# The sums of a modulation, once by VectorE over rows, once by TensorE over tiles

## The chip, the cores and the metric

One of the eight cores of a Trainium2 chip runs one launch of a layer of a streaming encoder, in fp32. The metric is the device time in microseconds (us) of a launch. The median of three runs of the kernel before is 1193.38 us.

## The reference

The layer has a token mixer (a convolution beside a gated recurrence) and a feed-forward part. Each is led by a normalisation whose shift and scale depend on a condition vector `c`. S = D = 1024, so that x has 8 x 8 tiles of 128 x 128.

```python
cond = jax.nn.silu(c)
mod = cond @ w_ada[l] + b_ada[l]          # 1024 -> 6 x 1024
sh1, sc1, gt1, sh2, sc2, gt2 = jnp.split(mod, 6)
h = rms_norm(x, g_pre_mix[l]) * (1.0 + sc1) + sh1
zin = h @ w_in[l]                         # 1024 x 1024 by 1024 x 3072
...
x = x + gt1 * rms_norm(mix, g_post_mix[l])
h2 = rms_norm(x, g_pre_ffn[l]) * (1.0 + sc2) + sh2
x = x + gt2 * rms_norm((silu(gate) * up) @ w_ffn_out[l], g_post_ffn[l])
```

The change is about `sh1` and `sc1`, 2 x 1024 sums of 1024 products each, for which 8 MB of `w_ada` are read.

## The kernel before

The program is written engine by engine, in one block; the order on every engine is that of its code, and semaphores are counted up between the engines. Every projection is made of three fp32r matmuls in place of one: weights and activations are split into a high and a low half (`w_hi`, `w_lo`, `ha_hi`, `ha_lo`, and `hb_` for the second half of the channels), and hi x hi, lo x hi and hi x lo are summed.

**The prologue** (until about 72 us) normalises x, transposes it, applies scale and shift, splits the result and makes the first two chunks of the input projection at the same time. It goes by sixteen groups: a group is a tile kt of 128 channels and a half of the tokens, in the order of `GROUPS` (line 71). For each of them

- TensorE transposes four tiles of x (`turn_x`, line 1443),
- ScalarE applies scale and shift out of PSUM into one of two buffers (line 663, the tile shows as `ggb`) and copies the high half (line 667),
- VectorE takes the low half (`low_half`, line 963), and
- TensorE makes six matmuls of 512 columns with it (`project_group`, line 1458).

TensorE's order is written out at the end of the tensor block: the transposes run three groups ahead of the projections.

**Scale and shift** come in four blocks of 256 channels. SyncE loads a block in four pieces of 512 KB (`load_block`, line 427) into a ring of three, so that the fourth block waits until the first is used. VectorE holds row p of channel group j on partition p: `sum_rows` multiplies the 512 values of a row j (256 shifts, 256 scales) by `cond[:, j]` and adds them up over j (lines 937 and 940), in two sums that line 945 adds (`acc_ready`). Then only the sum over the 128 partitions is left: `mod_sums(kt)` does it on TensorE with two matmuls against a column of ones (line 1430), for shift and scale of tile kt, and VectorE adds the bias and makes `gs` and `mod` from it (`scale_shift`, lines 952 and 954). VectorE's order is written out by hand, the pieces of `sum_rows` between the low halves.

**Others that look at these sums**: SyncE (the fourth block), and GpSimd, whose third split of weights (`split_at(2)`, lines 510 and 512) waits for the last block's sum. SyncE's later weight loads wait for the splits (line 396). GpSimd and SyncE then wait for the sixteenth group.

**Behind the prologue** TensorE makes the other chunks of the input projection (line 1495), with the heads' small matmuls and transposes between them, then the output projection and the feed-forward part (lines 1603 and 1680). The other four parts of the modulation are made there, on ScalarE and GpSimd, and summed over partitions by `column_sums` (line 1407); the change does not touch them.

Of the kernel before, what the change touches and what calls it, by code (L numbers as in the profile page):

```python
# [17 lines left out]
F32 = mybir.dt.float32  # L18
# [3 lines left out]
ALU = mybir.AluOpType  # L22
# [4 lines left out]
P = 128  # L27
D = 1024
S = 1024
KT = D // P  # L30
TT = S // P
# [38 lines left out]
ADA_RING = 3  # L70
# [69 lines left out]
def build(nc, t_in, out):  # L140
# [9 lines left out]
    with ctx:  # L150
        def sem(name):
            return ctx.enter_context(nc.semaphore(name))

        def group(specs):

            made = []
            with ExitStack() as place:
                for name, shape, dt in specs:
                    made.append(place.enter_context(nc.sbuf_tensor(name, shape, dt)))
            return made  # L160

        def keep(name, shape, dt=F32):
# [4 lines left out]
        ones = keep("ones", [P, P])  # L167
# [6 lines left out]
        cond = keep("cond", [P, KT])  # L174
# [20 lines left out]

        x0, ada0, acc0 = group([("x0", [P, TT, D], F32), ("ada0", [P, ADA_RING, KT, 2, 2 * P], F32),
                                      ("acc0", [P, 2, 2, 4 * P], F32)])
        qk, f, tt, vt, v, pmat, kdt, state, on, ot, y4, og, ada, acc, sg, u = group([
# [17 lines left out]
        def bank(i):  # L216
            return pair[i // 2][:, (i % 2) * HALF:(i % 2 + 1) * HALF]
# [12 lines left out]
        ada0_loaded = [sem(f"ada0_loaded{i}") for i in range(KT)]  # L230
        acc_ready = sem("acc_ready")
        full0_ready = sem("full0_ready")
# [157 lines left out]
        def _(sp):  # L390
# [31 lines left out]
            def load_block(b):  # L422
                if b >= ADA_RING:
                    sp.wait_ge(acc_ready, b - ADA_RING + 1)
                for q in range(4):
                    rows, s_ = slice(q // 2 * 4, q // 2 * 4 + 4), q % 2
                    sp.dma_start(ada0[:, b % ADA_RING, rows, s_, :], columns[:, rows, s_, b * 2 * P:(b + 1) * 2 * P]
                                 ).then_inc(ada0_loaded[2 * b + q // 2], 16)
# [54 lines left out]
        def _(pool):  # L483
# [51 lines left out]
            for g in range(2):  # L535
                split_at(g)
            pool.wait_ge(acc_ready, KT // 2)
            split_at(2)
# [355 lines left out]
        def _(dve):  # L894
# [33 lines left out]

            def sum_rows(b, rows):

                for j in rows:
                    src = ada0[:, b % ADA_RING, j, :, :].rearrange("p s n -> p (s n)")
                    dst = acc0[:, b % 2, j % 2, :]
                    if j % 4 == 0:
                        dve.wait_ge(ada0_loaded[2 * b + j // 4], 32)
                    if j < 2:
                        i_ = dve.tensor_scalar(dst, src, cond[:, j:j + 1], None, ALU.mult)
                    else:
                        me.wait(behind=1)
                        i_ = dve.scalar_tensor_tensor(out=dst, in0=src, scalar=cond[:, j:j + 1], in1=dst,  # L940
                                                      op0=ALU.mult, op1=ALU.add)
                    me.done(i_)
                if rows[-1] == KT - 1:
                    me.wait()
                    dve.tensor_tensor(acc0[:, b % 2, 0, :], acc0[:, b % 2, 0, :], acc0[:, b % 2, 1, :], ALU.add
                                      ).then_inc(acc_ready, 1)

            def scale_shift(kt):
# [22 lines left out]
            dve.wait_ge(cond_ready, 1)  # L971
            sum_rows(0, range(KT))
            for i in range(4):
# [5 lines left out]
            for i in range(5, TT):  # L979
                normalise_x(i)  # L980
            low_half(0)
            low_half(1)
            sum_rows(1, range(2))
            low_half(2)
            sum_rows(1, range(2, 4))
            low_half(3)
            sum_rows(1, range(4, KT))
            sum_rows(2, range(2))
            scale_shift(2)
            scale_shift(3)  # L990
            sum_rows(2, range(2, 4))
            low_half(4)
            sum_rows(2, range(4, 6))
            low_half(5)
            sum_rows(2, range(6, KT))
            low_half(6)
            scale_shift(4)
            low_half(7)
            sum_rows(3, range(3))
            scale_shift(5)  # L1000
            low_half(8)
            sum_rows(3, range(3, 6))
            low_half(9)
            sum_rows(3, range(6, KT))
            low_half(10)
            scale_shift(6)
            low_half(11)
            scale_shift(7)
            for g in range(12, 16):
# [385 lines left out]
        def _(pe):  # L1395
# [27 lines left out]
            def mod_sums(kt):  # L1423

                pe.wait_ge(acc_ready, kt // 2 + 1)
                if kt >= 2:
                    pe.wait_ge(full0_ready, 2 * kt - 3)
                for s_ in range(2):
                    first = s_ * 2 * P + kt % 2 * P
                    i_ = pe.matmul(bank(4 + 2 * (kt % 2))[:, s_:s_ + 1], acc0[:, kt // 2 % 2, 0, first:first + P],  # L1430
                                   ones[:, 0:1], start=True, stop=True)
                i_.then_inc(mod0_summed, 1)
# [352 lines left out]
```

## Time and profile before

| | |
|---|---|
| median of three runs | 1193.38 us (1192.98 to 1196.18) |
| profiled execution | 1198.91 us, span 1197.2 us |
| TensorE busy (matmuls) | 1149.7 us, 96% of the span |
| TensorE busy (weight loads) | 958.4 us, 80% |
| VectorE busy | 740.3 us, 62% |
| ScalarE, GpSimd busy | 306.0 us, 662.0 us |
| matmul records | 5528 |

The profiled execution has a time of its own, 1.7 us more than its span. TensorE counts as busy while a matmul runs, and matmuls overlap, so its busy share says little of its speed; the granted clock of a stretch (1.00 is 2.4 GHz, 0.50 is 1.2 GHz) stands beside it. A wait is put down to the instruction that ended it. The names in the profile are those of the tiles without their numbers: `ada` is `ada0`, `acc` is `acc0`, `pair` is PSUM.

### The profile page before, as it was taken

How to read it: one execution, taken by the hardware profiler on the slowest of the kernel's cores; microseconds unless marked ns; L12 is line 12 of the kernel's file. 1: busy time of each engine (PE TensorE's matmuls, PEld its weight loads, DVE VectorE, ACT ScalarE, POOL GpSimd, SP SyncE). 2: the span in 40 equal slices, each digit the busy share in tenths (PEclk: the TensorE clock that was granted, in tenths of full speed). 3: DMA queues.
4: the chain of work that ended last, by engine and by line, in shares of the span. 5: the costliest groups of instructions: out<-in, count | busy, mean ns of one | idle time of the engine just before them, and what ended most of it. 6: DMA issues, size and time to landing. Idle time of an engine off the chain costs nothing.

```text
span 1197.2 us, 13774 instructions
## 1 busy us (share of the span) xinstructions
PE 1149.7 (96%) x5528; PEld 958.4 (80%) x5528; DVE 740.3 (62%) x892; ACT 306.0 (26%) x459; POOL 662.0 (55%) x388
## 2 busy tenths in 40 slices
PE   2799999999999999999999999999999999999996
PEld 2678888888887888877888888888888888888875
DVE  6765988979988655658644444444444444444447
ACT  5355244272341624341110101010101010101014
POOL 4036433342433460324486868686868686868655
PEclk9999999999999999999999999999999999999988
DMA  9534323232310153211112121212120212121234
GB/s 331 165 123 141 97 87 93 81 102 71 104 37 24 49 206 110 88 36 53 36 34 72 34 73 35 71 35 72 34 72 27 79 35 72 35 71 35 71 116 184
DMA packets 94097, 98.52 MB, mean 82 GB/s; under 512 B 2925, under 2 KB 80978, under 8 KB 94034
## 3 DMA queue, kind: packets, MB, share of 16 engines
q1 hardware_dynamic: 92576, 93.33, 24.7%
q10 hardware_dynamic: 1458, 4.31, 0.9%
q8 instruction: 44, 0.72, 0.3%
q14 instruction: 19, 0.16, 0.0%
HBM read 89.25 MB, written 8.39 MB: 82 GB/s over the span
## 4 chain that ended last, share of the span: by engine, by line
PE 91%; DVE 5%; ACT 1%; SPq 1%; issue 1%; DMA 1%; ACTq 0%; DVEq 0%
PE pair L1680 30%; PE pair L1603 27%; PE pair L1495 22%; PE pair L1531 3%; PE pair L1458 1%; PE pair L1660 1%; DVE yt L1306 1%; DVE acc L940 1%; DMA x<-in_x 1%; SPq L396 1%; PE pair L1545 1%; PE pair L1526 1%; PE pair L1419 1%; PE pair L1407 1%; DVE yt L1310 1%
## 5 line engine op out<-in xcount | busy, mean ns | idle before, releaser
L1062 DVE SCALAR_TENSOR_TENSOR pair<-u,conv_w_col,pair 128x512 f32<-128x512 f32 x240 | 162.4, 747 | 1.2
L1360 DVE TENSOR_TENSOR yt<-yt,pair 128x1024 f32<-128x1024 f32 x80 | 97.6, 1220 | 101.8 <-PE pair L1603 101.2
L596 POOL TENSOR_TENSOR w_lo<-raw,w_hi 128x1024 fp32r<-128x1024 f32 x66 | 146.6, 2221 | 5.3
L594 POOL CAST w_hi<-raw 128x1024 fp32r<-128x1024 f32 x66 | 69.1, 1046 | 123.3 <-PE pair L1603 52.5
L517 POOL TENSOR_TENSOR w_lo<-raw,w_hi 128x1024 fp32r<-128x1024 f32 x21 | 52.4, 2496 | 106.3 <-ACT w_hi L681 106.3
L1603 PE MATMUL pair<-w_hi,u_hi 128*128 128x512 f32 x352 | 109.1, 391 | 0.0
L1603 PE MATMUL pair<-w_lo,u_hi 128*128 128x512 f32 x352 | 108.8, 390 | 0.0
L1603 PE MATMUL pair<-w_hi,u_lo 128*128 128x512 f32 x352 | 108.7, 390 | 0.0
L596 POOL TENSOR_TENSOR w_lo<-sraw,w_hi 128x1024 fp32r<-128x1024 f32 x38 | 104.2, 2742 | 3.0
L594 POOL CAST w_hi<-sraw 128x1024 fp32r<-128x1024 f32 x38 | 39.4, 1038 | 117.8 <-PE pair L1603 116.1
L528 POOL TENSOR_TENSOR acc<-acc,ada 128x1024 f32<-128x1024 f32 x28 | 67.3, 2403 | 52.4 <-ACT ada L725 51.1
L866 ACT ACTIVATE u_hi<-ufull 128x1024 fp32r<-128x1024 f32 x22 | 23.3, 1061 | 270.9 <-PE pair L1603 228.9
L1680 PE MATMUL pair<-t_hi,w_hi 128*128 128x512 f32 x228 | 88.7, 389 | 0.0
L1680 PE MATMUL pair<-t_lo,w_hi 128*128 128x512 f32 x228 | 88.7, 389 | 0.0
L1680 PE MATMUL pair<-t_hi,w_lo 128*128 128x512 f32 x228 | 88.7, 389 | 0.0
L1603 PEld LDWEIGHTS pair<-w_hi,u_hi 128*128 128x128 f32 x352 | 66.3, 189 | 14.0 <-DVE yt L1358 0.4
L1603 PEld LDWEIGHTS pair<-w_lo,u_hi 128*128 128x128 f32 x352 | 66.4, 188 | 13.9
L1603 PEld LDWEIGHTS pair<-w_hi,u_lo 128*128 128x128 f32 x352 | 66.3, 188 | 13.9
L1495 PE MATMUL pair<-ha_hi,w_hi 128*128 128x512 f32 x208 | 69.0, 413 | 4.2 <-ACT gate L842 2.3
L1495 PE MATMUL pair<-hb_hi,w_hi 128*128 128x512 f32 x208 | 68.1, 408 | 0.0
L1495 PE MATMUL pair<-ha_lo,w_hi 128*128 128x512 f32 x208 | 65.2, 395 | 0.0
L1495 PE MATMUL pair<-ha_hi,w_lo 128*128 128x512 f32 x208 | 65.0, 394 | 0.0
(255 smaller groups left out, 2591.1 us busy)
## 6 DMA issues: line engine op xcount, KB each, us to landing
ada<-in_w_ada SPq DMA_DIRECT2D x48, 512.0 KB, 4.0
raw<-in_w_ffn_in SPq DMA_DIRECT2D x44, 512.0 KB, 3.9
raw<-in_w_in SPq DMA_DIRECT2D x24, 512.0 KB, 3.9
raw<-in_w_ffn_out SPq DMA_DIRECT2D x22, 512.0 KB, 3.4
x<-in_x SPq DMA_DIRECT2D x8, 512.0 KB, 8.4
raw<-in_w_out SPq DMA_DIRECT2D x8, 512.0 KB, 3.4
x<-in_x SPq DMA_DIRECT2D x4, 1024.0 KB, 8.3
out<-x ACTq DMA_DIRECT2D x8, 512.0 KB, 2.6
```

Of the source, the lines that this page charges most:

```text
L396: sp.dma_start(raw[:, g % RAW, :] if src.shape[1] != KT else raw[:, g % RAW, :].rearrange("p (kt c) -> p kt c", kt=KT), src).then_inc(raw_ ...
L517: pool.tensor_tensor(w_lo[:, g % WS, :], raw[:, g % RAW, :], w_hi[:, g % WS, :], ALU.subtract).then_inc(w_split, 1)
L528: pool.tensor_tensor(acc[:, :], acc[:, :], ada[:, n % 2, :], ALU.add).then_inc(ada_added, 1)
L594: me.done(pool.tensor_copy(w_hi[:, g % WS, cols], src[:, cols]))
L596: pool.tensor_tensor(w_lo[:, g % WS, cols], src[:, cols], w_hi[:, g % WS, cols], ALU.subtract).then_inc(w_split, 1)
L866: act.activation(u_hi[:, e % 2, :], ufull[:, :], ACT.Copy).then_inc(uhi_ready, 1)
L1062: i_ = dve.scalar_tensor_tensor(out=dst, in0=src, scalar=w, in1=dst, op0=ALU.mult, op1=ALU.add)
L1360: dve.tensor_tensor(yt[:, i, :], yt[:, i, :], pair[2 + i % 2][:, :], ALU.add).then_inc(y_added, 1)
L1495: i_ = pe.matmul(dst[:, cols], w, x[:, cols], start=first and s_ == 0, stop=last and s_ == 2)
L1531: i_ = pe.matmul(dst[0:rows, i * 64:(i + 1) * 64], qk[:, 1, i * P:i * P + rows], right(qk[:, 0, cols(i)], 1 << half), start=True, stop=True)
L1603: i_ = pe.matmul(dst[:, cols], x, w[:, cols], start=first and s_ == 0, stop=last and s_ == 2)
L1680: i_ = pe.matmul(dst, a, x[:, n, :], start=n == 0 and s_ == 0, stop=n == 3 and s_ == 2)
```

## The change

`sum_rows` goes, and with it the tile `acc0` and the semaphore `acc_ready`. `mod_sums(kt)` now reads the loaded block itself: for the shift and for the scale of tile kt it adds up eight matmuls in PSUM, one for each j, with the 128 x 128 tile of `ada0` as weights and the column `cond[:, j]` moving. It waits for the block's loads in place of `acc_ready`. The fourth load and GpSimd's third split wait for `mod0_summed`, that is for TensorE. The two other steps of VectorE keep their order.

```diff
             def load_block(b):
                 if b >= ADA_RING:
-                    sp.wait_ge(acc_ready, b - ADA_RING + 1)
+                    sp.wait_ge(mod0_summed, 2 * (b - ADA_RING + 1))
...
             for g in range(2):
                 split_at(g)
-            pool.wait_ge(acc_ready, KT // 2)
+            pool.wait_ge(mod0_summed, KT)
             split_at(2)
...
-            def sum_rows(b, rows):
...
-            sum_rows(0, range(KT))
             for i in range(4):
                 normalise_x(i)
...
-            low_half(0)
-            low_half(1)
-            sum_rows(1, range(2))
-            low_half(2)
-            sum_rows(1, range(2, 4))
...
+            for g in range(4):
+                low_half(g)
             scale_shift(2)
             scale_shift(3)
...
+            for g in range(4, 12):
+                low_half(g)
+                if g % 2:
+                    scale_shift((g + 3) // 2)
...
             def mod_sums(kt):
 
-                pe.wait_ge(acc_ready, kt // 2 + 1)
+                b = kt // 2
                 if kt >= 2:
                     pe.wait_ge(full0_ready, 2 * kt - 3)
+                for n in range(2):
+                    pe.wait_ge(ada0_loaded[2 * b + n], 32)
                 for s_ in range(2):
-                    first = s_ * 2 * P + kt % 2 * P
-                    i_ = pe.matmul(bank(4 + 2 * (kt % 2))[:, s_:s_ + 1], acc0[:, kt // 2 % 2, 0, first:first + P],
-                                   ones[:, 0:1], start=True, stop=True)
+                    for j in range(KT):
+                        i_ = pe.matmul(bank(4 + 2 * (kt % 2))[:, s_:s_ + 1], ada0[:, b % ADA_RING, j, s_, kt % 2 * P:kt % 2 * P + P],
+                                       cond[:, j:j + 1], start=j == 0, stop=j == KT - 1)
                 i_.then_inc(mod0_summed, 1)
```

TensorE's order between the third group and the fifth, before; line 1430 is `mod_sums` of tiles 2 and 3, line 1458 the projections, line 1443 the transposes:

```order
L1458 MATMUL pair<-ha_hi,w_hi 128x512
L1458 MATMUL pair<-ha_lo,w_hi 128x512
L1458 MATMUL pair<-ha_hi,w_lo 128x512
L1430 MATMUL pair<-ones,acc 128x1 x4
L1458 MATMUL pair<-ha_hi,w_hi 128x512
L1458 MATMUL pair<-ha_lo,w_hi 128x512
L1458 MATMUL pair<-ha_hi,w_lo 128x512
L1458 MATMUL pair<-ha_hi,w_hi 128x512
L1458 MATMUL pair<-ha_lo,w_hi 128x512
L1458 MATMUL pair<-ha_hi,w_lo 128x512
L1443 MATMUL pair<-ident,x 128x128 x12
```

and with the change, where these are lines 1390, 1418 and 1403:

```order
L1418 MATMUL pair<-ha_hi,w_hi 128x512
L1418 MATMUL pair<-ha_lo,w_hi 128x512
L1418 MATMUL pair<-ha_hi,w_lo 128x512
L1390 MATMUL pair<-cond,ada 128x1 x32
L1418 MATMUL pair<-ha_hi,w_hi 128x512
L1418 MATMUL pair<-ha_lo,w_hi 128x512
L1418 MATMUL pair<-ha_hi,w_lo 128x512
L1418 MATMUL pair<-ha_hi,w_hi 128x512
L1418 MATMUL pair<-ha_lo,w_hi 128x512
L1418 MATMUL pair<-ha_hi,w_lo 128x512
L1403 MATMUL pair<-ident,x 128x128 x12
```

The place is the same; 4 matmuls of one column have become 32. For the later tiles, one at a time, 2 become 16.

VectorE's order from the first low half on, before (line 937, 940 and 945 are `sum_rows`, 952 and 954 `scale_shift`):

```order
L963 TENSOR_TENSOR ha_lo<-ggb,ha_hi 128x512 x2
L937 TENSOR_SCALAR acc<-ada,cond 128x512 x2
L963 TENSOR_TENSOR ha_lo<-ggb,ha_hi 128x512
L940 SCALAR_TENSOR_TENSOR acc<-ada,cond,acc 128x512 x2
L963 TENSOR_TENSOR ha_lo<-ggb,ha_hi 128x512
L940 SCALAR_TENSOR_TENSOR acc<-ada,cond,acc 128x512 x4
L945 TENSOR_TENSOR acc<-acc 128x512
L937 TENSOR_SCALAR acc<-ada,cond 128x512 x2
L952 SCALAR_TENSOR_TENSOR gs<-pair,scale_bias,vec 128x1
L954 TENSOR_TENSOR mod<-pair,vec 128x1
L952 SCALAR_TENSOR_TENSOR gs<-pair,scale_bias,vec 128x1
L954 TENSOR_TENSOR mod<-pair,vec 128x1
```

and with the change, where `low_half` is line 942 and `scale_shift` lines 931 and 933:

```order
L942 TENSOR_TENSOR ha_lo<-ggb,ha_hi 128x512 x4
L931 SCALAR_TENSOR_TENSOR gs<-pair,scale_bias,vec 128x1
L933 TENSOR_TENSOR mod<-pair,vec 128x1
L931 SCALAR_TENSOR_TENSOR gs<-pair,scale_bias,vec 128x1
L933 TENSOR_TENSOR mod<-pair,vec 128x1
L942 TENSOR_TENSOR ha_lo<-ggb,ha_hi 128x512 x2
L931 SCALAR_TENSOR_TENSOR gs<-pair,scale_bias,vec 128x1
L933 TENSOR_TENSOR mod<-pair,vec 128x1
```

Between the low halves only the small steps of `scale_shift` are left.

## Rows read from the trace of the kernel before

**Rows 1.** The page, chain that ended last: shares of the span by engine.
```profile
PE 91%; DVE 5%; ACT 1%; SPq 1%; issue 1%; DMA 1%; ACTq 0%; DVEq 0%
```

**Rows 2.** Waits of TensorE, 29 to 74 us: total, times, longest.
```profile
PE pair L1430 <- DVE acc L945: 4.9, 3, 2.3
PE pair L1495 <- ACT sg L692: 1.9, 1, 1.9
PE pair L1458 <- DVE ha_lo L963: 1.4, 1, 1.4
```

**Rows 3.** Stretches: length, busy us (instructions) per engine, clock, DMA share, GB/s.
```profile
29.00:72.00 43.00, 36.75 (x171) 29.59 (x169) 28.72 (x59) 21.39 (x31) 4.64 (x3) 0.92 0.46 138
46.00:48.00 2.00, 2.00 (x13) 1.72 (x13) 0.47 (x3) 1.19 (x2) 0.00 (x0) 0.88 0.03 8
48.00:50.00 2.00, 2.00 (x8) 1.68 (x7) 1.74 (x4) 0.77 (x2) 0.00 (x0) 0.50 0.00 0
50.00:52.00 2.00, 2.00 (x11) 1.64 (x10) 0.46 (x2) 0.86 (x2) 0.00 (x0) 0.77 0.00 0
58.00:60.00 2.00, 2.00 (x9) 1.81 (x10) 0.35 (x3) 0.67 (x1) 1.92 (x2) 0.50 0.00 0
```

**Rows 4.** Timeline: start, us, engine, operation; the sums over partitions (line 1430).
```profile
13.47 1.78 PEld L1430 LDWEIGHTS pair<-ones,acc 128*128 128x128 f32 x8 [6.42 <-DVE acc L945]
...
36.44 1.05 PE L1430 MATMUL pair<-ones,acc 128*128 128x1 f32 x8 [0.66 <-DVE acc L945]
...
37.35 0.48 PE L1458 MATMUL pair<-ha_hi,w_hi 128*128 128x512 f32 x1
...
45.64 0.60 PE L1430 MATMUL pair<-ones,acc 128*128 128x1 f32 x4 [2.30 <-DVE acc L945]
...
57.52 0.82 PE L1430 MATMUL pair<-ones,acc 128*128 128x1 f32 x4 [1.90 <-DVE acc L945]
```

**Rows 5.** Timeline of TensorE: projections at 30 and 35 us.
```profile
30.25 0.63 PE L1458 MATMUL pair<-ha_hi,w_lo 128*128 128x512 f32 x1
30.68 0.63 PE L1458 MATMUL pair<-ha_hi,w_hi 128*128 128x512 f32 x1
...
34.69 0.39 PE L1458 MATMUL pair<-ha_hi,w_lo 128*128 128x512 f32 x1
34.92 0.40 PE L1458 MATMUL pair<-ha_hi,w_hi 128*128 128x512 f32 x1
```

**Rows 6.** The tile ada, to 60 us: ns min/median/max, first and last start.
```profile
L940 DVE SCALAR_TENSOR_TENSOR acc<-ada,cond,acc x24: 737/746/752, 8.5 to 56.0; 128x512 f32<-128x512 f32 x24
```

**Rows 7.** Timeline: transposes of x, the fifth tile, the copies, the last normalisation.
```profile
19.91 1.97 PE L1443 MATMUL pair<-ident,x 128*128 128x128 f32 x8 [4.57 <-DVE mod L954]
...
22.47 0.93 DVE L926 TENSOR_SCALAR x<-x,rs 128x1024 f32<-128x1024 f32 x1
...
23.74 1.90 DVE L910 TENSOR_TENSOR lb_tmp<-vec 128x4 f32<-128x4 f32 x1
...
27.46 0.75 DVE L926 TENSOR_SCALAR x<-x,rs 128x1024 f32<-128x1024 f32 x1
```

**Rows 8.** Timeline of TensorE: sixteen one-column records (line 1407) among projections.
```profile
126.44 1.84 PE L1407 MATMUL pair<-ones,acc 128*128 128x1 f32 x16
128.14 0.72 PE L1495 MATMUL pair<-ha_hi,w_hi 128*128 128x512 f32 x2
```

**Rows 9.** The tile ada, to 3 us: the first block's loads and landings.
```profile
L427 SPq DMA_DIRECT2D ada<-in_w_ada x4: 434/500/519, 0.8 to 2.4; - x4
...
DMA to landing us min/median/max: 4.2/5.8/7.5
```

**Rows 10.** Timelines of GpSimd and of SyncE's queue.
```profile
57.66 1.30 POOL L510 CAST w_hi<-raw 128x1024 fp32r<-128x1024 f32 x1 [32.05 <-DVE acc L945]
...
17.37 18.15 SPq L427 DMA_DIRECT2D ada<-in_w_ada  x12
...
35.65 26.23 SPq L396 DMA_DIRECT2D raw<-in_w_in  x3
```

More of the change, by code:

```diff
@@ L193, in build @@
         hb_lo = keep("hb_lo", [P, 4, S], F32R)
-        x0, ada0, acc0 = group([("x0", [P, TT, D], F32), ("ada0", [P, ADA_RING, KT, 2, 2 * P], F32),
-                                      ("acc0", [P, 2, 2, 4 * P], F32)])
+        x0, ada0 = group([("x0", [P, TT, D], F32), ("ada0", [P, ADA_RING, KT, 2, 2 * P], F32)])
         qk, f, tt, vt, v, pmat, kdt, state, on, ot, y4, og, ada, acc, sg, u = group([
@@ L230, in build @@
         ada0_loaded = [sem(f"ada0_loaded{i}") for i in range(KT)]
-        acc_ready = sem("acc_ready")
         full0_ready = sem("full0_ready")
@@ L926, in normalise @@
                 return dve.tensor_scalar(dst, src, rs[:, which, col:col + 1], None, ALU.mult)
-            def sum_rows(b, rows):
[L931 to L946, printed above, removed]
             def scale_shift(kt):
@@ L980, in _ @@
                 normalise_x(i)
-            low_half(0)
-            low_half(1)
-            sum_rows(1, range(2))
-            low_half(2)
-            sum_rows(1, range(2, 4))
-            low_half(3)
-            sum_rows(1, range(4, KT))
-            sum_rows(2, range(2))
+            for g in range(4):
+                low_half(g)
             scale_shift(2)
             scale_shift(3)
[L991 to L1008, printed above, removed]
+            for g in range(4, 12):
+                low_half(g)
+                if g % 2:
+                    scale_shift((g + 3) // 2)
             for g in range(12, 16):
```

## The prediction

> **What bounds the kernel now.** I read the chain of waits first, as shares of the span [rows 1]: TensorE holds 91% of it and VectorE, which makes the sums that the change moves, 5%. So the change can only matter where TensorE waits for these sums, and where it gets more work. I then asked who TensorE waited for between 29 and 74 us, the first projections [rows 2]: 4.9 us in three waits for the last addition of a sum (line 945), 1.4 us for VectorE's low half (line 963), and 1.9 us behind the prologue, for ScalarE's first evacuation. The table of stretches [rows 3] shows what else the waits cost. From 29 to 72 us TensorE is busy for 36.75 of 43 us, and its granted clock stands at 0.50, which is 1.2 of 2.4 GHz, in 48 to 50 us and in 58 to 60 us. Each time it fell after a wait: the engine stood still for 2.30 us before 45.64 and for 1.90 us before 57.52 [rows 4]. The clocks of the three stretches from 46 to 52 us (0.88, 0.50, 0.77) put 0.5 + 2.0 + 0.9 = 3.4 us at half clock there, and I take the same for the second. The wait of 1.9 us behind the prologue is no part of this change. For the beginning the matmuls tell it: projections start 0.43 us apart at 30 us and 0.23 us apart at 34.7 us [rows 5], so the engine began at 1.2 GHz. From 73.9 us on, TensorE runs nearly without a break, so whatever the prologue gains or loses by then arrives whole at the end.
>
> **The change, part by part.** Against the profiled execution (span 1197.2, time 1198.9 us) I sum differences alone, and apply them to the median of 1193.4 us. That execution is 0.5% slower than the median; none of the terms below is long enough for that to matter.
>
> *VectorE loses its sums.* Eight steps for each of four blocks; the 24 fused ones among them take 0.746 us each [rows 6], 17.9 us, and with the first two steps and the last addition of each block it is somewhat over 20 us of busy time. Only TensorE's waits for them are on the path: 4.9 us in the projections. The wait of 6.4 us before 13.47 [rows 4] is not: after it TensorE still waits for normalised x, whose fifth tile is done at 23.4 us because its load lands late [rows 7]. The wait of 1.4 us for line 963 stays as well, since it is the way from a transpose over ScalarE's two passes and VectorE's low half, with the sums beside it. So **-4.9 us**.
>
> *TensorE gets them.* A tile of the modulation had two matmuls of one column, and now has sixteen. Each shows as two records (8 records for the 4 instructions of the first two tiles [rows 4]), so a tile goes from 4 to 32 records. The time of one is that of its weight load, as the moving side has one column. In the steady part sixteen such records take from 126.44 to the next matmul at 128.14 us, 0.106 each, at full clock [rows 8]; at half clock eight took 1.78 us, 0.22 each [rows 4]. At full clock a tile is then 32 x 0.106 = 3.4 us in place of 0.46 (8 records from 36.44 to 37.35 us for two tiles), 2.94 more. Two of the eight tiles lie at the start, in idle time. Six lie between the projections, where TensorE is what the others wait for: 6 x 2.94 = **+17.6 us**. Nothing covers this: with VectorE's sums gone, TensorE is the only full engine there.
>
> *The start.* The first block's four loads are issued up to 2.4 us and land after 4.2 to 7.5 us, so the last is there at 9.9 us [rows 9]. Two tiles then take 64 x 0.22 = 14.1 us at half clock and end at 24.0, or at about 17 us if the clock rises. VectorE has the scale and shift of both tiles ahead of the fifth normalisation, and the small transposes that it copies afterwards stand behind eight transposes of x on TensorE (1.97 us now, then about 0.8 us for the small ones [rows 7]). In the slow case that gives 24.2 + 2.0 + 0.8 = 27.0, the copies to 27.5, three normalisations at 0.86 us, their pitch now, to 30.1, against 28.2 now. I take 1.7 us, since part of the copies' present 2.3 us was a wait beside GpSimd that falls away; the ends are 0 and 2.
>
> *The clock in between.* This is the term that no row of before prices. During a tile's sums TensorE is loading weights and streams almost nothing. What the rows show is that it fell after waits of 2.3 and 1.9 us with a tile's sum right behind each, 4 records of one column [rows 3, 4]. These sums did not keep it up, while the wait of 1.4 us for line 963, with projections and transposes around it, did not bring it down. From two falls I take it that sums do not hold the clock as projections do. Then a run of 3.4 us of loads brings the clock down in the middle of it, and it needs projections to come back, about 3.4 us as in both rows. A tile's cost is then between nothing (the tile is over first) and 5.1 us (3.4 of the loads doubled, 1.7 of the recovery); no row is nearer to one end, so I take the middle, 2.55. Six tiles are 15.3; tiles 2 and 3 stand back to back and share a recovery, 1.7 less: **+13.6 us**. The two half-clock stretches of now (2 x 1.7) belong to the waits that go: **-3.4 us**.
>
> *Queues.* The loads of the fourth block now wait for TensorE's second tile (24 us in place of 13.4). That queue's first load of this block is the ninth of twelve between 17.37 and 35.5 us, so about 29 us: no cost. GpSimd's third split waited for the last sum and ran from 57.66 us until shortly before 61.9, when the load behind it went out; it now waits for all eight tiles, which are done five projections (7 us or more) before the third chunk begins, against about 4 us of work. SyncE's next weight load, which waits for that split, would come some 4 us after the last tile; it is wanted two chunks, some 20 us, later [rows 10]. I cost both at nothing. If that cover were gone, the third chunk would wait for at most those 4 us.
>
> Sum: 17.6 - 4.9 + 13.6 - 3.4 + 1.7 = **+24.6 us, 1218.0 us**.
>
> **The rivals.**
> *The clock stays up.* If the clock stays at full speed over the sums, the terms are 17.6 - 4.9 - 3.4 = +9.3 us, 1202.7 us, with 1201 to 1205 around it (one fall may remain). For it: the weight-load engine would be fuller than ever. Against it: the two falls, each with a sum's records before it.
> *Half clock throughout.* If the projections between the tiles are too short to bring it back, each tile costs the whole 5.1 us: 17.6 - 4.9 + 30.6 - 3.4 + 1.7 = +41.6, 1235 us. Two projections and two transposes lie between two tiles, 3.7 us at full clock and 7 at half, and the rows show it coming back within 3.4 us, so this is unlikely.
> *The loads hide.* TensorE may load weights beside a running matmul: a projection's load vanishes in a pace of 0.23 us [rows 5]. If the sums' loads slid beside the 512-column matmuls before them or into the waits for ScalarE, the sums would cost less than before. The turning point against 4.9 + 3.4 = 8.3 us of gain is 6 x (32 p - 0.46) = 8.3, p = 0.058 us for a record; at p = 0 the time is 1193.4 - 8.3 - 2.8 = 1182.3 us, faster. Against it stands the pace of 0.106 for sixteen in a row, in the middle of dense projections [rows 8]: a queue of loads has nothing to hide behind but itself.
> The Trainium skill (TensorE: Matmul & The Clock Gate, section Back-to-back issue gap) gives matmuls of 1 to 64 columns an issue floor of about 25 ns, or about 62 ns where the sequencer decodes. As an estimate by that page, 62 ns would give 6 x (2.0 - 0.46) - 8.3 = +0.9 us, no change, and 25 ns 6.3 us less; the trace's 106 ns decides against both.
>
> **How the numbers follow.** Half clock around the sums 0.65 (+24.6); clock up 0.27 (+9.3); half throughout 0.04; loads hidden 0.03; 0.01 for what I have not seen. The likeliest case alone spans a tile's clock cost of 1.2 to 3.6 us and a start of 0 to 2: +16 to +32, 1209 to 1226. The range reaches down to the case with the clock up, so 1201 to 1226. A change under 0.3% (3.6 us) can't be told from none. Both main cases are above that: slower 0.96, same 0.02, faster 0.02, the last two from the hidden loads.
>
> **What the next profile would show.** The matmuls of one column: 256 records, against 32; 0.106 us apart at full clock, 0.21 at half. The waits of line 1430 for line 945 gone, with no wait of TensorE over 1.5 us between the first projection and the last. The granted clock at 0.50 around the sums, five or six times between 37 and 95 us: that is the step most open, and if the column shows 1.00 there, the time is near 1203. The prologue's last projection ends at about 96 us, against about 72. VectorE's busy time falls by over 20 us without effect. From then on the two traces should run in parallel; if the difference at the end is not that of the prologue, the claim that it arrives whole is wrong. If the third chunk waits for GpSimd's split, the queue term is.

## The result, and the profile after

| | before | changed |
|---|---|---|
| median of the runs | 1194.83 us (5 runs, 1192.98 to 1196.18) | 1219.85 us (5 runs, 1217.93 to 1222.1) |
| ratio, 95% interval | | 1.0208 (1.0192 to 1.0224) |
| profiled execution: span | 1197.2 us | 1220.2 us |
| TensorE, matmul records | 5528 | 5752 |
| VectorE busy | 740.3 us | 719.2 us |
| first projection of the prologue | 29.25 us | 30.00 us |
| third chunk's first matmul | 73.91 us | 96.84 us |

The change makes the kernel 25 us slower; forecast were 24.6 us and 1218.0 us. The profiled executions (1198.91 and 1221.93 us) lie 4.1 and 2.1 us above their medians. The difference of their spans is 23.0 us, and that of the third chunk's start, the first work behind the prologue, is 22.93 us. What follows takes 1123.29 us before and 1123.36 us after, so the loss is made in the prologue and arrives whole. TensorE's timeline before, and below it with the change; the first line of each pair is the eighteenth projection, the last work ahead of the sums of the second block, the other begins the third chunk:

```profile
35.38 0.40 PE L1458 MATMUL pair<-ha_hi,w_lo 128*128 128x512 f32 x1
...
73.91 0.70 PE L1495 MATMUL pair<-ha_hi,w_hi 128*128 128x512 f32 x2 [1.89 <-ACT sg L692]
```

```profile
35.41 0.39 PE L1418 MATMUL pair<-ha_hi,w_lo 128*128 128x512 f32 x1
...
96.84 0.70 PE L1455 MATMUL pair<-ha_hi,w_hi 128*128 128x512 f32 x2 [1.89 <-ACT sg L690]
```

The whole loss, 22.90 us of it, is made between these two places.

Who TensorE waited for in the prologue, in the changed kernel (total, times, longest), beside [rows 2]:

```profile
PE pair L1455 <- ACT sg L690: 1.9, 1, 1.9
PE pair L1418 <- DVE ha_lo L942: 0.8, 1, 0.8
PE pair L1418 <- DVE hb_lo L942: 0.5, 1, 0.5
PE pair L1403 <- DVE x L924: 0.4, 1, 0.4
```

The three waits for VectorE's sums, 4.9 us, are gone, and what came in their place is small. The low half's wait is 0.8 us instead of 1.4, with 0.5 us once more at the end and 0.4 us for a normalised tile of x that falls just behind 29 us. Its granted clock, by stretches (columns as in [rows 3]):

```profile
29.00:95.00 66.00, 64.67 (x341) 57.61 (x341) 15.53 (x33) 21.54 (x31) 4.71 (x3) 0.79 0.31 92
36.00:40.00 4.00, 4.00 (x38) 4.00 (x37) 0.28 (x2) 0.00 (x0) 0.00 (x0) 0.99 1.09 348
40.00:44.00 4.00, 4.00 (x21) 4.00 (x20) 0.00 (x0) 0.00 (x0) 0.00 (x0) 0.50 1.14 310
64.00:68.00 4.00, 4.00 (x18) 3.81 (x19) 0.88 (x3) 0.74 (x1) 0.00 (x0) 0.50 0.00 0
82.00:86.00 4.00, 4.00 (x36) 3.92 (x36) 0.04 (x1) 0.55 (x1) 0.00 (x0) 1.00 0.00 0
```

From 29 to 95 us TensorE is busy for 64.67 of 66 us, and the mean clock is 0.79 against 0.92 in 29 to 72 us before. Time at half clock is twice what is missing to 1.00, so (1 - 0.79) x 66 = 13.9 us were lost to it, against (1 - 0.92) x 43 = 3.4 us. The same from stretches of 2 us, which round less, is 13.6 us, in four falls: 5.1 us between 39 and 51 us, 1.7 between 56 and 61, 3.4 between 63 and 71 and 3.4 between 74 and 81. After 81 us the clock stays at 1.00 to the prologue's end. The sums themselves in TensorE's timeline, beside [rows 4] and [rows 8]:

```profile
9.78 13.78 PE L1390 MATMUL pair<-cond,ada 128*128 128x1 f32 x64 [2.30 <-DMA ada<-in_w_ada]
...
35.63 9.75 PE L1390 MATMUL pair<-cond,ada 128*128 128x1 f32 x64
45.25 0.77 PE L1418 MATMUL pair<-ha_hi,w_hi 128*128 128x512 f32 x1
...
52.76 3.63 PE L1390 MATMUL pair<-cond,ada 128*128 128x1 f32 x32
56.25 0.64 PE L1403 MATMUL pair<-ident,x 128*128 128x128 f32 x4
...
61.52 4.75 PE L1390 MATMUL pair<-cond,ada 128*128 128x1 f32 x32
66.13 1.09 PE L1403 MATMUL pair<-ident,x 128*128 128x128 f32 x4
...
71.91 4.87 PE L1390 MATMUL pair<-cond,ada 128*128 128x1 f32 x32
76.64 1.09 PE L1403 MATMUL pair<-ident,x 128*128 128x128 f32 x4
...
82.29 3.63 PE L1390 MATMUL pair<-cond,ada 128*128 128x1 f32 x32
85.78 0.63 PE L1403 MATMUL pair<-ident,x 128*128 128x128 f32 x4
```

A tile's 32 records take 3.49 us where the clock stays up (52.76 to 56.25, 82.29 to 85.78), 0.109 us each. At 61.52 and 71.91 us the clock falls within them, and they take 4.6 and 4.7 us. The pair at 35.63 us takes 9.62 us: full clock to about 40 us, then half. Each of the four falls came within a tile's sums or just behind them, and from 36 to 81 us the engine stood still only once, for 0.8 us, so the falls did not need a wait. The first 64 records run at half clock throughout, 13.64 us to the transposes at 23.42, 0.213 each.

### The profile page after: what moved, and what is told of

It is laid out like the page before. It is cut to its first block, busy times and chain, and to the rows that moved or that the text cites. A ratio compares the mean times of both kernels' runs of the same rounds, so it can differ in the third digit from the quotient of the medians.

```text
span 1220.2 us, 14184 instructions
## 1 busy us (share of the span) xinstructions
PE 1188.7 (97%) x5752; PEld 997.6 (82%) x5752; DVE 719.2 (59%) x856; ACT 306.0 (25%) x459; POOL 662.2 (54%) x388
## 3 DMA queue, kind: packets, MB, share of 16 engines
q10 hardware_dynamic: 1458, 4.31, 0.9%
HBM read 89.25 MB, written 8.39 MB: 80 GB/s over the span
## 4 chain that ended last, share of the span: by engine, by line
PE 93%; DVE 4%; ACT 1%; issue 1%; DMA 1%; SPq 0%; ACTq 0%; DVEq 0%
PE pair L1640 29%; PE pair L1563 26%; PE pair L1455 22%; PE pair L1491 3%; PE pair L1390 3%; PE pair L1418 2%; PE pair L1620 1%; DVE yt L1264 1%; PE pair L1403 1%; DMA ada<-in_w_ada 1%; PE pair L1505 1%; PE pair L1486 1%; PE pair L1377 1%; PE pair L1365 1%; DVE yt L1268 1%
## 5 line engine op out<-in xcount | busy, mean ns | idle before, releaser
L1563 PEld LDWEIGHTS pair<-w_hi,u_lo 128*128 128x128 f32 x352 | 66.4, 188 | 13.9
L1563 PEld LDWEIGHTS pair<-w_lo,u_hi 128*128 128x128 f32 x352 | 66.4, 189 | 13.9
```

The lines of the kernel that those rows point to most:

```text
L1563: i_ = pe.matmul(dst[:, cols], x, w[:, cols], start=first and s_ == 0, stop=last and s_ == 2)
```

## The experiments

The times are medians, each beside that of the kernel before on the same chip, with the ratio's 95% interval. They are set beside TensorE's places in the profiled executions. The start of the third chunk leaves out what varies in the 1120 us behind it: that rest was 1118.8 to 1123.4 us, with no relation to the edits. The way from the eighteenth projection to the third chunk also leaves out the beginning, where x arrives at other times and where the clock, at half as in [rows 5], rose after up to ten projections. The same instructions up to there took 5.15 us from the first projection to the eighteenth in one kernel and 5.88 us in another, so this is no effect of the edits. Starts in us:

| kernel | first projection | eighteenth | third chunk | eighteenth to third chunk |
|---|---|---|---|---|
| before | 29.25 | 35.38 | 73.91 | 38.53 us |
| the change | 30.00 | 35.41 | 96.84 | 61.43 |
| 64 columns | 30.45 | 35.60 | 84.82 | 49.22 |
| one row | 30.39 | 36.38 | 66.80 | 30.42 |
| 64 columns, half the rows | 29.29 | 35.44 | 73.92 | 38.48 |
| 8 columns | 29.97 | 35.28 | 90.35 | 55.07 |
| 128 columns | 28.84 | 34.24 | 83.67 | 49.43 |
| one block, 64 columns | 31.01 | 36.04 | 71.97 | 35.93 |
| the same again | 28.97 | 34.15 | 70.07 | 35.92 |
| one block, one column | 29.30 | 34.99 | 74.87 | 39.88 |
| 64 columns, early split | 30.65 | 36.53 | 85.85 | 49.32 |
| 64 columns, first block by VectorE | 29.20 | 34.73 | 83.94 | 49.21 |
| one block, dropped matmuls | 29.48 | 33.46 | 69.39 | 35.93 |
| the same again | 29.43 | 34.45 | 70.37 | 35.92 |

### The clock apart from the loads: 64 columns

```diff
-                dve.scalar_tensor_tensor(out=gs[:, 0, kt:kt + 1], in0=sums[:, 1:2], scalar=scale_bias[:, kt:kt + 1],
+                dve.scalar_tensor_tensor(out=gs[:, 0, kt:kt + 1], in0=sums[:, 64:65], scalar=scale_bias[:, kt:kt + 1],
...
-                        i_ = pe.matmul(bank(4 + 2 * (kt % 2))[:, s_:s_ + 1], ada0[:, b % ADA_RING, j, s_, kt % 2 * P:kt % 2 * P + P],
-                                       cond[:, j:j + 1], start=j == 0, stop=j == KT - 1)
+                        i_ = pe.matmul(bank(4 + 2 * (kt % 2))[:, s_ * 64:(s_ + 1) * 64], ada0[:, b % ADA_RING, j, s_, kt % 2 * P:kt % 2 * P + P],
+                                       cond[:, j:j + 1].to_broadcast([P, 64]), start=j == 0, stop=j == KT - 1)
```

> The change with one edit: each of the sixteen matmuls of a tile streams 64 equal columns (the condition's column repeated) in place of one, and VectorE reads the first. The same 256 records and weight loads. Theory (the clock falls because the sums stream almost nothing): weight loads set the pace, so a tile still takes 32 x 0.107 = 3.4 us at full clock, and the granted clock stays at 1.00 between the first tiles 2 and 3 and the prologue's end; the 13.6 us of half clock go, and the kernel is 9 to 11 us slower than before, near 1205, and about 15 us faster than the change. Rival 1 (the clock falls in any run of weight loads, whatever they stream): no difference from the change, +25 us against before. Rival 2 (64 columns cost time of their own): slower than the change.

1205.68 us against 1194.98: +10.7 us, ratio 1.0081 (1.0061 to 1.0101); eighteenth projection to third chunk 49.22 us, 12.2 us less than in the change. The number of instructions, of weight loads and the order are those of the change; only what streams through the array differs. Two stretches of this kernel:

```profile
36.00:40.00 4.00, 4.00 (x38) 4.00 (x38) 0.28 (x2) 0.00 (x0) 0.00 (x0) 1.00 1.09 348
48.00:52.00 4.00, 4.00 (x34) 3.83 (x33) 0.49 (x1) 1.07 (x2) 0.00 (x0) 1.00 0.02 6
```

and its sums in TensorE's timeline:

```profile
10.25 13.89 PE L1390 MATMUL pair<-cond,ada 128*128 128x64 f32 x64 [2.91 <-DMA ada<-in_w_ada]
...
35.82 7.25 PE L1390 MATMUL pair<-cond,ada 128*128 128x64 f32 x64
...
48.73 3.68 PE L1390 MATMUL pair<-cond,ada 128*128 128x64 f32 x32
```

From 34 us to the prologue's end the clock stays at 1.00. The pair takes 7.25 us and each tile 3.68 us with its overlap; from a tile's start to the next instruction it is 3.51 us, against 3.49 with one column. The theory holds, and both rivals fall. Of the change's 25 us, the clock is 12 (profiled executions) to 14 (medians).

### The gain side alone: one row

```diff
-                    for j in range(KT):
+                    for j in range(1):
...
-                                       cond[:, j:j + 1], start=j == 0, stop=j == KT - 1)
+                                       cond[:, j:j + 1], start=j == 0, stop=j == 1 - 1)
```

> The change, with the sum over only the first of the eight channel groups j; the other seven are left out of shift and scale. A tile has its 4 records again, as before, and VectorE has no sums: this is the gain side alone. Theory: the waits of 4.9 us go and with them the two half-clock stretches, 3.4 us; with the sums out of the way 7 to 9 us faster than before. Rival (the waits for VectorE hid others, of ScalarE or of the low halves, that come out at once): within 2 us of before.

1186.77 us against 1194.98: -8.2 us, ratio 0.9926 (0.9909 to 0.9943). The third chunk comes 7.1 us earlier, in an execution in which ScalarE got the fifth tile of x 1.2 us later; the eighteenth projection to the third chunk is 30.42 us, 8.1 us less. So the two negative terms together, 4.9 + 3.4 = 8.3 us, are what VectorE's sums cost. The clock column reads 1.00 (the column doesn't show the beginning at half clock, here as before), and TensorE waits for the low half as long as before. The stretch of the prologue:

```profile
29.00:66.00 37.00, 33.65 (x174) 27.91 (x173) 16.01 (x34) 23.57 (x34) 4.71 (x3) 1.00 0.60 181
```

That wait, in the table of TensorE's waits:

```profile
PE pair L1418 <- DVE ha_lo L942: 1.4, 1, 1.4
```

### The price of a load: half the rows

As with 64 columns, `for j in range(4)`.

> As the run with 64 columns, with the sum over four of the eight channel groups; the other four are left out. 16 records for a tile instead of 32. Against the run with 64 columns it has 16 records fewer in each of the six tiles between the projections. Theory (a record costs 0.106 us of TensorE on the path): 6 x 16 x 0.106 = 10.2 us faster than that run, so within 2 us of before (6 x (1.7 - 0.46) - 8.3 = -0.9). Rival (records are partly hidden beside projections once they are fewer): 3 us or more faster than before.

1195.50 us against 1194.98, ratio 1.0005 (0.9994 to 1.0016); eighteenth projection to third chunk 38.48 us, against 49.22 with all rows. That is 10.74 us for 96 records fewer: 0.112 us each. Nothing is hidden beside the projections. A tile's 16 records take 1.89 us in TensorE's timeline, about half of 3.68:

```profile
44.98 1.89 PE L1390 MATMUL pair<-cond,ada 128*128 128x64 f32 x16
```

### Eight columns, and 128

The same edit with 8 and with 128 in place of 64.

> The change with 8 columns streamed in place of 1 (64 in the earlier run). If it is the streamed columns that hold the clock, 8 should be close to 1: half clock around the sums again, 20 to 25 us slower than before. If it was the repeated-column operand as such, or the place of the result in PSUM, that held it, 8 does as well as 64: about 11 us slower than before.

1214.48 us against 1194.43: +20 us, ratio 1.017 (1.0141 to 1.02), between the change and 64 columns, as is the way to the third chunk, 55.07 us. In the profiled execution, which was its fastest, the clock fell in the pair of tiles and once more between 56 and 60 us, and stayed up over the last three tiles. Two stretches:

```profile
40.00:44.00 4.00, 4.00 (x21) 4.00 (x20) 0.00 (x0) 0.00 (x0) 0.00 (x0) 0.50 1.14 306
56.00:60.00 4.00, 4.00 (x19) 3.31 (x18) 1.58 (x4) 1.41 (x2) 0.00 (x0) 0.59 0.00 0
```

The four executions ran from 1212.5 to 1221.5 us, wide like those of the early split below (1204.6 to 1214.7 us). So the operand as such and the place in PSUM are excluded (8 columns have both and the clock falls), and eight columns hold it in some places and not in others. The expectation "close to one column" was too simple.

> The change with 128 columns streamed. In the run with 64, the clock held at full speed between the projections, but the 64 records at the start ran at 0.217 us each, half clock, for 13.9 us without raising it. Theory A (more columns raise it too): the start's records fall to about 0.11 us each within the first 7 us; the time is that of 64 columns or 1 to 2 us less. Theory B (they do not): as with 64 columns, 10 to 12 us slower than before. If 128 columns cost time of their own: more than 0.11 us for a record at full clock, 12 us or more slower.

1206.33 us against 1194.34: +12.0 us, ratio 1.0095 (1.0069 to 1.0121); eighteenth projection to third chunk 49.43 us, as with 64 columns (49.22). 128 columns cost next to no time of their own: the pair takes 7.06 us to the next instruction, 0.110 us for a record, as with 64, and a tile 3.57 us against 3.51. Theory A held at the start: the 64 records took 9.63 us in place of 13.7, so the clock rose within them, which it had not done with 64 columns. TensorE's timeline at the start:

```profile
9.87 9.76 PE L1390 MATMUL pair<-cond,ada 128*128 128x128 f32 x64 [2.62 <-DMA ada<-in_w_ada]
19.50 1.16 PE L1403 MATMUL pair<-ident,x 128*128 128x128 f32 x8
...
28.84 0.78 PE L1418 MATMUL pair<-ha_hi,w_hi 128*128 128x512 f32 x1
29.41 0.63 PE L1418 MATMUL pair<-ha_lo,w_hi 128*128 128x512 f32 x1
```

The full clock did not last to the projections: TensorE stood still for x (2.2 and 2.8 us), the clock fell at 25 us, and the first projections were at half clock again (28.84 to 29.41 us). The sums' earlier end did: the first projection begins 8.32 us after ScalarE gets the fifth tile of x, against 9.86 us with 64 columns. The medians don't show it.

### TensorE for one block only

In the kernel before, the second block (tiles 2 and 3) by TensorE with the change's matmuls and 64 columns (`BY_TILES` is `(1,)`), the others by VectorE. Its pieces are put anew:

```diff
+                if b in BY_TILES:
+                    ...
...
-            low_half(0)
-            low_half(1)
-            sum_rows(1, range(2))
...
+            for g in range(4):
+                low_half(g)
+            sum_rows(2, range(KT))
+            scale_shift(2)
+            scale_shift(3)
+            sum_rows(3, range(5))
+            low_half(4)
...
```

> The kernel before, where only the second block (tiles 2 and 3) is summed by TensorE, with 64 columns; VectorE sums blocks 0, 2 and 3, with its pieces put anew between the low halves. Theory: TensorE gets 64 - 8 records, 5.9 us; VectorE is relieved of 5.7 us just where its sums were late, so that the waits of 4.9 us and the two half-clock stretches of 3.4 us go: -2.4 us against before, 1 to 3 us faster. Rival (VectorE is late again with blocks 2 and 3): waits for line 945 of 1 us or more stay, and it is 2 to 6 us slower than before.

1192.16 us against 1194.98: -2.8 us, ratio 0.9975 (0.9963 to 0.9986). The same kernel ran again later:

> TensorE sums the second block alone, with 64 columns: the same kernel as before in this series, to stand beside the run with dropped matmuls on the same chip. 2 to 3 us faster than the kernel before.

1192.21 us against 1194.34: -2.1 us, ratio 0.9981 (0.997 to 0.9992). The eighteenth projection to the third chunk is 35.93 and 35.92 us, against 38.53 before: 2.6 us less, where 2.4 was expected. No wait for line 947, the last addition there, is left, and the clock is at 1.00 in the stretch of the prologue:

```profile
29.00:72.00 43.00, 39.17 (x231) 33.66 (x231) 25.99 (x54) 24.98 (x36) 4.99 (x3) 1.00 0.55 167
```

TensorE's waits in this kernel:

```profile
PE pair L1501 <- ACT sg L694: 1.9, 1, 1.9
PE pair L1464 <- DVE ha_lo L965: 1.4, 1, 1.4
```

With one column in place of 64:

> As the run where TensorE sums the second block alone, with one column streamed in place of 64. Theory: the run of 64 weight loads at 36 us, 6.8 us, brings the clock down in its middle, as in the change, and it comes back some 3.4 us of projections later; tiles 2 and 3 cost 5 us more than with 64 columns (3.4 us of loads doubled, 1.7 of recovery), so about 1.5 to 3 us slower than before. Rival (the clock fell in the change because of its later, single tiles): no difference from the run with 64 columns, 2 to 3 us faster than before.

1196.47 us against 1194.43: +2.0 us; the ratio 1.0009 (0.9998 to 1.0021) doesn't tell it from before, and tells it from 64 columns. The eighteenth projection to the third chunk is 39.88 us, 3.95 us more than with 64 columns; expected were 5. The clock itself cost 5.1 us, and the wait for the low half is 0.6 us in place of 1.4. The stretches from 36 to 52 us:

```profile
36.00:40.00 4.00, 4.00 (x37) 4.00 (x36) 3.18 (x6) 0.00 (x0) 0.00 (x0) 0.97 1.09 348
40.00:44.00 4.00, 4.00 (x20) 4.00 (x20) 0.59 (x3) 0.00 (x0) 0.00 (x0) 0.50 1.13 311
48.00:52.00 4.00, 3.45 (x16) 2.83 (x15) 2.02 (x3) 3.56 (x6) 0.00 (x0) 0.75 0.00 0
```

The loads begin at 35.22 us; the clock is down from about 40 to 50 us. One run of 64 such records brings it down by itself, as in the change.

### The queue term

With 64 columns, GpSimd's split early:

```diff
-            pool.wait_ge(mod0_summed, KT)
+            pool.wait_ge(mod0_summed, KT // 2)
```

> The change with 64 columns, where GpSimd's third split waits for the fourth tile's sums in place of the eighth's. Theory (the delay of that split and of the weight load behind it is covered): the same as the run with 64 columns, 10 to 11 us slower than before. Rival (it costs something, since the split and the next chunk's load come 30 us later than before): 2 us or more faster than that run. Third possibility: the split now runs beside VectorE's low halves and slows them, up to 1 us slower.

1208.78 us against 1194.43: +14.4 us, ratio 1.0119 (1.0083 to 1.0154), and four executions from 1204.6 to 1214.7 us: the medians don't tell it from the run with 64 columns. By the traces the two are the same: 49.32 us from the eighteenth projection to the third chunk, against 49.22. Under this sum two waits traded places. The split now runs beside a pair of low halves, and TensorE's wait for them is 2.3 us instead of 1.4; that wait did not bring the clock down. VectorE's timeline:

```profile
47.40 2.18 DVE L942 TENSOR_TENSOR ha_lo<-ggb,ha_hi 128x512 fp32r<-128x512 f32 x2 [3.07 <-ACT ha_hi L665]
```

and GpSimd's:

```profile
46.08 2.35 POOL L510 TENSOR_TENSOR w_lo<-raw,w_hi 128x1024 fp32r<-128x1024 f32 x1
```

The other wait is at the prologue's end. There the late split stretches VectorE's last low halves, and TensorE waits 0.5 us for one, with 64 columns as in the change; with the early split these low halves take 0.68 and 0.69 us and the wait is gone. In the change:

```profile
86.12 1.04 POOL L508 CAST w_hi<-raw 128x1024 fp32r<-128x1024 f32 x1 [60.88 <-PE pair L1390]
...
86.16 1.54 DVE L942 TENSOR_TENSOR hb_lo<-ggb,hb_hi 128x512 fp32r<-128x512 f32 x1
...
90.56 0.50 PE L1418 MATMUL pair<-hb_hi,w_hi 128*128 128x512 f32 x1 [0.49 <-DVE hb_lo L942]
```

So neither place of the split is free, and the difference between them is 0.1 us.

### The start

VectorE sums the first block again, TensorE the others with 64 columns.

> The change with 64 columns, except that VectorE sums the first block over rows as before; TensorE sums blocks 1 to 3. Theory: the two tiles at the start lie in idle time but for their tail (scale and shift of the second tile hold up VectorE's fifth normalisation), so the first projection begins 8.3 us after ScalarE gets the fifth tile of x, as before, against 9.1 us in the change and 9.9 us with 64 columns; about 1.5 us faster than the run with 64 columns, so 8 to 10 us slower than before. Rival (the first block's sums on TensorE cost nothing at all): the same as that run.

1204.61 us against 1194.34: +10.3 us, ratio 1.0085 (1.0068 to 1.0102): the medians don't tell it from the run with 64 columns (1.0081). In the traces, ScalarE gets the fifth tile of x at 20.92 us and the first projection begins at 29.20, 8.28 us later, against 8.39 before, 9.14 in the change and 9.86 with 64 columns. The tail of the first block's sums is real, 0.75 us in the change. But it does not reach the sums of the second block: the eighteenth projection begins 14.52 us after that tile before and 14.55 us in the change (15.01 with 64 columns, 13.81 here), because the clock rose after seven projections in the change and after ten before.

### A warm start

The last point of the clock is not the change's: the first projections ran at half clock in every kernel so far. Seven matmuls of 512 columns with dropped results fill TensorE's waits for x, in the kernel with one block by TensorE:

```diff
+            def warm(n):
+                pe.wait_ge(w_split, 1)
+                for _ in range(n):
+                    pe.matmul(pair[0][:, 0:HALF], w_hi[:, 0, 0:P], w_hi[:, 0, 0:HALF], start=True, stop=True)
...
                 for i in range(4):
+                    if g == 2 and i:
+                        warm(5 if i == 1 else 1)
                     pe.wait_ge(xs_ready, 4 * half + i + 1)
```

> As the run where TensorE sums the second block alone with 64 columns, with seven matmuls of 512 columns whose results are dropped, put into TensorE's waits for the last four tiles of x (24 to 28 us), so that it streams there. Theory (the clock was at half until 33 us because TensorE stood still before the projections): the first projections start at full clock, about 2 us faster than that run, 4 to 5 us faster than before. Rival (seven are too few, or they push the transposes back): no gain, or up to 1 us slower than that run.

1191.78 us against 1194.43, ratio 0.9973 (0.9963 to 0.9984).

> The same with the seven dropped matmuls. Its trace showed the first projections at full clock (0.23 us apart from 29.8 us on), but its median was that of the kernel without them within 0.4 us, on another chip. Theory (the gain is real, the chips differed): 1.5 to 2.5 us faster than the run without them. Rival (what the early projections gain is waited for later or lost at the transposes, or the clock is not up in every execution): within 1 us.

1191.81 us against 1192.21 of the kernel without them on the same chip: 0.4 us, less than the medians can tell. The rival holds, by its last part. The first kernel's profiled execution had the projections 0.23 us apart from 29.81 us on; the second's, of the same code, at 30.01 us still 0.42 us apart. TensorE's timeline of the first:

```profile
24.16 2.48 PE L1443 MATMUL pair<-w_hi 128*128 128x512 f32 x5
...
29.81 0.39 PE L1471 MATMUL pair<-ha_lo,w_hi 128*128 128x512 f32 x1
30.04 0.40 PE L1471 MATMUL pair<-ha_hi,w_lo 128*128 128x512 f32 x1
```

and of the second:

```profile
23.75 2.48 PE L1443 MATMUL pair<-w_hi 128*128 128x512 f32 x5
...
30.01 0.63 PE L1471 MATMUL pair<-ha_lo,w_hi 128*128 128x512 f32 x1
30.43 0.63 PE L1471 MATMUL pair<-ha_hi,w_lo 128*128 128x512 f32 x1
```

Where the clock was up, the gain was kept: the eighteenth projection begins 11.95 us after ScalarE gets the fifth tile of x in the first of these, and 13.42 us in the second, against 13.35 and 13.46 us without the dropped matmuls, and from there to the third chunk all four take 35.92 or 35.93 us. Two executions don't say how often it happens.

The fastest kernels that compute the whole layer are these two, with and without the dropped matmuls, 2 to 3 us under the kernel before.

## Why the prediction was right

**Where the loss arrives.** Right: 22.93 of 23.0 us are there when the third chunk begins.

**VectorE's waits, -4.9, and their clock, -3.4.** Right in sum, 8.3: 8.2 us faster with one row left, 8.1 in its trace. No run parts the two. The wait of 1.4 us for the low half stayed, as argued, where the clock was up (1.4 us with one row and with 64 columns).

**The loads, +17.6.** Slightly too small. The price of a record was 0.106 us from one row of 16; in runs of 32 and more it is 0.109, so that six tiles are 6 x (3.49 - 0.46) = 18.2 us. The sum of this term and the two before was +9.3 us, and the kernel with 64 columns, where the clock stays up, is 10.7 us slower, by its median and from the eighteenth projection to the third chunk alike. So the rest is not the start. The dearer records (0.8 us there) and the wait of 0.5 us beside the late split are most of it. The rival of hidden loads is refuted by the half of the rows, 0.112 us for each record less.

**The clock, +13.6.** Right in mechanism and in total, not tile by tile. The forecast took the middle of 0 and 5.1 us for a tile, for lack of a row: 2.55 for a single tile, 3.4 for the pair that shares a recovery. The falls cost 5.1 us with the pair, 1.7, 3.4 and 3.4 us with three single tiles and nothing with the last, 13.6 in all. In the first single tile the clock held over the loads and fell right behind them, at 57 us. That the total came so near is luck; that it lay between 5 and 20 us was the argument. The ground for it was weaker than it sounds: in the kernel before, the clock also fell behind the third chunk's start, after the wait of 1.9 us, with no sum near:

```profile
76.00:78.00 2.00, 2.00 (x7) 1.52 (x6) 2.00 (x5) 1.74 (x2) 2.00 (x2) 0.50 0.00 0
```

So the rows of before could not tell a sum's records from the wait ahead of them. The runs can: with the same loads and 64 columns streaming, the clock stays at 1.00.

**The start, +1.7.** The one term that was wrong. The first projection begins 0.75 us later, and by the eighteenth nothing of it is left (35.41 against 35.38 us), since the clock rose three projections earlier; the forecast had no term for that. Of the 0.75 us: I had put the fifth normalisation, the transposes and the copies one behind the other. The normalisation took 1.80 us beside GpSimd's split, in place of 0.93, until 25.79 us; the transposes ran beside it and were done by then, and the three small instructions behind it, of which the last took 1.90 us before [rows 7], took 0.20, 0.28 and 0.16 us. VectorE was slow beside GpSimd's split in both kernels, each time in another of its instructions. Its timeline in the change:

```profile
23.99 1.80 DVE L924 TENSOR_SCALAR x<-x,rs 128x1024 f32<-128x1024 f32 x1
25.79 0.20 DVE L904 COPY vec<-pair 128x41 f32<-128x41 f32 x1
...
26.21 0.16 DVE L908 TENSOR_TENSOR lb_tmp<-vec 128x4 f32<-128x4 f32 x1
...
26.49 0.75 DVE L924 TENSOR_SCALAR x<-x,rs 128x1024 f32<-128x1024 f32 x1
```

**The queues, 0.** Right for the waits that it weighed: the split ran at 86.12 us, after GpSimd had stood idle for 60.9 us, and the third chunk waited for ScalarE alone, 1.9 us as before. What it left out is what the split does to VectorE while it runs, which cost TensorE 0.5 us.

**The sum.** With what the profile shows, 18.2 - 4.9 + 13.6 - 3.4 = 23.5 us against 22.9 measured. Of the 0.6 us left, 0.5 are in the waits: a wait is counted from the modelled end of the matmul before it, while the three gaps for VectorE's sums, from 0.23 us (a projection's pace) after the start of the last projection, are 5.4 us. The other 0.1 is the low half's shorter wait with the new one beside the split. Of the forecast's 24.6 us, 1.7 (the start) did not come, and 0.6 more came from the loads. The bounds of the likeliest case, +16 to +32, are by its own terms +15 to +31; nothing hangs on it.

**The signs that were named.** 256 records, 0.109 and 0.213 us apart; the waits gone; no wait over 1.5 us between the projections; last projection from 94.56 to 94.95 us, forecast about 96; VectorE 21 us less busy. The clock fell four times between 37 and 95 us, not five or six.

On the price of a load: the floors of 25 or 62 ns for 1 to 64 columns that the prediction took from the Trainium skill (TensorE: Matmul & The Clock Gate, section Back-to-back issue gap) stand there for a single matmul, without a weight load. For pairs of a load and a matmul of 128 columns the section gives about 81 ns; this case has 110 ns for such a record in fp32. The same page's section LDWEIGHTS (loading the stationary operand) gives the columns of the weights over 1.2 GHz, 107 ns for 128 as an estimate by it, and that agrees with the trace at full clock (109 ns); at half clock the trace has 213 ns, for which the section has no word.

## What to carry to other kernels

A sum over rows that is moved to TensorE as tiles times one column costs a weight load for each 128 x 128 tile, which shows twice in fp32 (256 records for 128 matmuls here), and on an engine that is already the full one this is paid whole; ask what the moved work weighs on the receiving engine before asking what it frees. If such a run is needed, try a repeated column as the moving side: 64 of them cost no time beside the load here (3.51 against 3.49 us for a tile) and gave back 12 to 14 of 25 us. And move only as much as the late engine is late by: one block of four turned the loss into a small gain.

## What the runs showed that was not expected

- With 64 repeated columns a high clock held over runs of 3.5 to 7 us of sums, but a low one did not rise: at the start the 64 records ran at half clock to their end, 13.7 us. With 128 columns they took 9.63 us, and a record in the pair was no longer than with 64. Eight columns gave executions from 1212.5 to 1221.5 us.
- With matmuls of 512 columns in the waits ahead of the projections the clock was up there in one profiled execution and not in the other, at the same instruction order, and the medians saw neither.
- The same wait of 1.9 us ahead of the third chunk was followed by a fall of the clock in five profiled executions (mean 0.72 over the next 6 us, before and in the change, with half the rows, with 8 columns and with the early split) and by none in the other nine. What decides it is open.
- The part behind the prologue varied by 4.6 us between profiled executions of kernels whose code is the same there. A difference of spans of one pair of executions would have said that one row in place of eight gains 11.6 us; the start of the third chunk said 7.1 us, the medians 8.2 us and the way from the eighteenth projection 8.1 us.
